# Reading the moving operand from the last column to the first in the three-product matmuls of a hybrid decoder layer

## What is computed

```python
h = rms_norm(x)                       # (512, 1024)
z = h @ w_in                          # w_in: 1024 x 6696, columns of all heads and of four gates
o_a, o_b, o_c, o_d = sparse attention, pooling, gated chunks, stick-breaking attention   # 256 wide each
proj = einsum('bsnw,nwd->bsnd', stack(o), w_branch)
x = x + sum_n(sigmoid(gate_n) * proj_n) @ w_out
h = rms_norm(x)
x = x + (silu(h @ w_ffn_gate) * (h @ w_ffn_up)) @ w_ffn_down      # 2816 hidden channels
```

## Time and profile before

| | us |
|---|---|
| median of 3 runs (773.85 to 774.11) | 774.07 |
| span of the profiled execution, first to last instruction | 772.3 |
| PE busy / PEld busy | 767.1 / 680.1 |
| DVE busy | 564.4 |
| ACT busy | 392.0 |
| POOL busy | 102.4 |
| chain that ended last: PE's share | 98% |

### The profile page before, as it was taken

How to read it: one execution, slowest core, us unless ns; L and a number is a source line. 1 busy time by engine, 2 the same in 40 slices (tenths; PEclk the granted TensorE clock), 3 DMA queues, 4 the chain that set the end, 5 groups by cost and what they waited for, 6 DMA issues and landing times.

```text
span 772.3 us, 11546 instructions
## 1 busy us (share of the span) xinstructions
PE 767.1 (99%) x4582; PEld 680.1 (88%) x4582; DVE 564.4 (73%) x796; ACT 392.0 (51%) x589; POOL 102.4 (13%) x126
## 2 busy tenths in 40 slices
PE   8999999999999999999999999999999999999998
PEld 8988888888888888888888899999889999999886
DVE  5536988878788965334435799889989888887991
ACT  6645545356573564443334465555544555555430
POOL 7100040457203211211310000000000000000000
PEclk9999999999999999999999999999999999999999
DMA  8362213221223221513234054335073333338202
GB/s 276 105 190 71 93 55 110 84 82 55 69 95 109 68 96 56 218 55 112 107 129 152 20 179 146 101 98 217 0 250 110 106 110 110 109 109 284 98 28 82
DMA packets 66629, 87.72 MB, mean 114 GB/s; under 512 B 1988, under 2 KB 52496, under 8 KB 66576
## 3 DMA queue, kind: packets, MB, share of 16 engines
q1 hardware_dynamic: 65680, 85.86, 34.0%
q0 software_dynamic: 752, 0.99, 0.5%
q10 hardware_dynamic: 144, 0.13, 0.0%
HBM read 81.21 MB, written 4.19 MB: 111 GB/s over the span
## 4 chain that ended last, share of the span: by engine, by line
PE 98%; issue 1%; POOL 1%; ACT 0%; DVE 0%; DVEq 0%; POOLq 0%
PE bank L2054 17%; PE bank L2056 17%; PE bank L2055 17%; PE bank L2499 9%; PE bank L2501 9%; PE bank L2500 9%; PE bank L2564 5%; PE bank L2560 5%; PE bank L2562 5%; PE bank L2327 1%; PE bank L2162 1%; PE bank L2297 1%; PE bank L2286 1%; PE bank L2318 1%; PE bank L2234 1%
## 5 line engine op out<-in xcount | busy, mean ns | idle before, releaser
L2054 PE MATMUL bank<-h_hi,w_hi 128*128 128x512 f32 (+1 forms) x368 | 139.9, 380 | 0.1
L2056 PE MATMUL bank<-h_hi,w_lo 128*128 128x512 f32 (+1 forms) x368 | 138.2, 376 | 0.0
L2055 PE MATMUL bank<-h_lo,w_hi 128*128 128x512 f32 (+1 forms) x368 | 138.1, 375 | 0.0
L1317 DVE TENSOR_TENSOR w_lo<-raw,w_hi 128x2048 fp32r<-128x2048 f32 x36 | 84.8, 2360 | 53.7 <-ACT w_hi L774 45.8
L2499 PE MATMUL bank<-t_hi,w_hi 128*128 128x256 f32 x320 | 89.6, 280 | 0.0
L2501 PE MATMUL bank<-t_hi,w_lo 128*128 128x256 f32 x320 | 89.4, 279 | 0.0
L2500 PE MATMUL bank<-t_lo,w_hi 128*128 128x256 f32 x320 | 89.4, 279 | 0.0
L2056 PEld LDWEIGHTS bank<-h_hi,w_lo 128*128 128x128 f32 x368 | 69.2, 188 | 12.8
L2054 PEld LDWEIGHTS bank<-h_hi,w_hi 128*128 128x128 f32 x368 | 69.2, 188 | 12.5 <-issue 0.4
L2055 PEld LDWEIGHTS bank<-h_lo,w_hi 128*128 128x128 f32 x368 | 69.3, 188 | 12.2
L774 ACT ACTIVATE w_hi<-raw 128x2048 fp32r<-128x2048 f32 x34 | 65.2, 1923 | 15.6 <-PE bank L2056 14.4
(11 more groups left out here) (305 smaller groups left out, 1804.5 us busy)
## 6 DMA issues: line engine op xcount, KB each, us to landing
raw<-in_w_in_dram SPq DMA_DIRECT2D x26, 1024.0 KB, 5.1
raw<-in_w_ffn_gate_dram SPq DMA_DIRECT2D x11, 1024.0 KB, 5.2
raw<-in_w_ffn_up_dram SPq DMA_DIRECT2D x11, 1024.0 KB, 5.2
raw<-in_w_ffn_down_dram SPq DMA_DIRECT2D x7, 1024.0 KB, 4.9
raw<-in_w_branch_dram SPq DMA_DIRECT2D x4, 1024.0 KB, 4.9
raw<-in_w_out_dram SPq DMA_DIRECT2D x4, 1024.0 KB, 4.8
b<-in_w_ffn_down_dram SPq DMA_DIRECT2D x4, 1024.0 KB, 6.7
x_sb<-in_x_dram SPq DMA_DIRECT2D x4, 512.0 KB, 6.2
```

The costliest lines, as they stand in the source:

```text
L1317: vec.tensor_tensor(w_lo[:, at], raw[:, c % 2, 0:n], w_hi[:, at].bitcast(F32), ALU.subtract)\
L2054: mm(dst, l_hi, r_hi, start=start, stop=False)
L2055: mm(dst, l_hi, r_lo, start=False, stop=False)
L2056: return mm(dst, l_lo, r_hi, start=False, stop=stop)
```

## The change

`three` turns the destination and the moving operand round, where the moving operand has two dimensions (so not in `pair_tile`), and `down_stage` does the same in its own three matmuls. Column 511 is read first and column 0 last, and column j of the product still lands in column j of PSUM. The stationary operand is as before, and so are all waits, counts, transfers and other engines' work. `wino_chunk` is not touched.

```diff
             def three(dst, l_hi, l_lo, r_hi, r_lo, start, stop):
 
+                if len(r_hi.shape) == 2:
+
+                    dst, r_hi, r_lo = dst[:, ::-1], r_hi[:, ::-1], r_lo[:, ::-1]
                 mm(dst, l_hi, r_hi, start=start, stop=False)
                 mm(dst, l_hi, r_lo, start=False, stop=False)
                 return mm(dst, l_lo, r_hi, start=False, stop=stop)
@@
                             w = slice(w_at(c) + k * HALF, w_at(c) + (k + 1) * HALF)
-                            mm(bank[banks[t]][:, :], l_hi[:, k, rows], w_hi[:, w], start=anew and k == 0, stop=False,
+                            mm(bank[banks[t]][:, ::-1], l_hi[:, k, rows], w_hi[:, w][:, ::-1], start=anew and k == 0,
+                               stop=False, skip_group_check=True)
+                            mm(bank[banks[t]][:, ::-1], l_hi[:, k, rows], w_lo[:, w][:, ::-1], start=False, stop=False,
                                skip_group_check=True)
-                            mm(bank[banks[t]][:, :], l_hi[:, k, rows], w_lo[:, w], start=False, stop=False,
-                               skip_group_check=True)
-                            ins = mm(bank[banks[t]][:, :], l_lo[:, k, rows], w_hi[:, w], start=False,
+                            ins = mm(bank[banks[t]][:, ::-1], l_lo[:, k, rows], w_hi[:, w][:, ::-1], start=False,
                                      stop=k == tiles - 1, skip_group_check=True)
                         ins.then_inc(S["down_tile"], 1)
```

## The result

| | before | after |
|---|---|---|
| median, us | 773.96 (4 runs) | 784.56 (4 runs) |
| ratio, 95% interval | | 1.0136 (1.0122 to 1.0151) |
| span of the profiled execution, us | 772.3 | 782.6 |

The change makes the kernel 10.6 us slower. The page of after, against the earlier trace rows: PE has 10.2 us more of busy time, the clock is as full as before and the chain lies on PE for 99% (98% before).

What follows compares the result with a forecast made beforehand. PE was taken as the bound, through distances between instruction starts. 1878 x 6 = 11.3 us plus 432 x 1.8 = 0.8 gave 12.1 off the 772.3 span; with 1.8 outside it, 762 us, range 749 to 797.

Steps and rivals of the forecast that it cites:

- the second rival: Turned matmuls: reads running the same way stay together longer; +8 ns on 2310, 18 us, 792; half, 783; chance 0.18.
- What bounds the kernel: Whole kernel: PE busy 767.1 of 772.3 us, so time is the sum of distances between its instruction starts.
- no other engine takes part: First down stage is tightest: 1.3 us saved there against DVE's 3.9 free, so the whole gain reaches the end.
- The count: Matmuls turned in `three` and the down stages: 1878 of 512 columns, 426 us, and 432 of 256, 52 us.
- the term for 512 columns: 1878 turned matmuls in `three` and the down stages: -6 ns each from 227, 11.3 us saved.
- The term for 256 columns: 432 turned matmuls by `three`: from 120 to the seven-product chunks' 118.2 ns, -1.8 each, 0.8 us saved.
- Nothing changes: Turned matmuls: the 32 cycles are a constant price of changing weights, or the order isn't carried out; 774; chance 0.27.
- Much slower: Turned matmuls: downward read or write falls to half pace, 427 ns for 512 columns; +446 us, 1220; chance 0.12.
- faster, by 2 to 25 us: Whole kernel: the likeliest case, time 762, own range given as 747 to 772, chance 0.43.
- the bound for 256 columns: Turned matmuls of 256 columns: distance no lower than the 107 ns of a weight load, at most -13 ns.

Runs made afterwards that it cites:

- e8: The kernel before, all reads upward, with `h` moved by 192 bytes against everything else; 778.65 us, ratio 1.0061.
- the rows: Separate kernels, layer not computed, running rows of equal matmuls in various lays and read directions; 512 columns upward at distance 0 took 226.6 ns, downward 233.4.
- second kernel of rows: Rows again, layer not computed, with lays in 16-byte steps and 512 columns read by blocks; blocks of 64 backwards, each upward: 226.6 ns.
- first kernel of rows: Rows of 32 equal matmuls, layer not computed, varying lay in 64-byte steps, direction, width and stationary columns; 512 columns: up 226.6 ns, down 233.4.
- third kernel of rows: Rows of 256 columns upward in the seven-product chunks' operand order, after short rows of another kind; the same row took 117.7, 113.3 and 117.9 ns.
- e3: The kernel before, all upward, with f and t laid so seven-product weights start 64 bytes after the moving operand; 772.87 us, ratio 0.9976.

## Why the prediction was wrong

The forecast was 762 us, faster; it came out 784.6, slower and inside the stated range. It is the second rival, a little slower.

*What bounds the kernel* was right: PE alone, 98% before and 99% after, and the time is the sum of the distances. So was the statement that no other engine takes part: PE's waits grew by 0.2 us.

*The count* was right: 1878 turned matmuls of 512 columns and 432 of 256; their sums moved by 11.0 and -0.2 us, and the seven products by less than 0.2.

*The step that failed* is the sign of the term for 512 columns: -6 ns each, 11.3 us saved, where +5.9 in the mean and +6.6 in the steady stretches was measured, 11.0 us lost. The prediction reasoned that a weight load read from the last column and a moving operand turned the same way have one pass over each other in place of three, and so fewer meetings. That the place of the weights matters to the moving read was right for the upward one, and e8 and the rows show it; that one can count passes was a picture with nothing behind it. No row of a trace shows the direction of a weight load either; the prediction has it from the compiled instruction list. The second kernel of rows contradicts it: the moving operand read by blocks of 64 columns from the end runs downward over the whole tile, with the pattern of every 256 bytes kept, and costs nothing. And the excess doesn't shrink when a weight load reads a quarter of the columns. The term for 256 columns, -1.8, came out at -1.6 in the first kernel of rows (120.0 and 118.4) and at -0.5 over the layer's 432, 0.2 us in place of 0.8. The right sign there is luck, since it came from the same reasoning.

What should have carried more weight stood in the front of this text: the tiles were laid so that weights and moving operand start alike, and the one pair of 512 columns with another lay had 235 ns. The rival took its +8 ns from there. The indexer's weights start 64 bytes after its moving operand, and upward rows at 64 have 233.1 ns with no semaphore between, so some 6.5 of the 8 were the lay's. The rows say that the upward lay at 0 is one of three good ones in sixteen, so a change of the order of the read, with no reason why it should be good at 0 too, should have been expected to lose. The rival's size was close for 512 columns, but it had a loss for 256 as well, and there the change gave a little back.

*Nothing changes* rested on 13.3 ns for both widths as a constant. Upward at a distance of 0 it is one, for a third width too (384 columns, L108: 5.55/32 = 173.4 ns, 13.4 above their 160.0), but it doesn't hold for another lay or order, as the rows from 226.6 to 240 ns show. *Much slower*, half pace for a downward read, is out: 233.4 ns. "PSUM — Partial Sum Buffer" (Specifications) of the Trainium skill was weighed there with its sentence on non-contiguous patterns; with the write alone downward the time is 773.93 us, so a step of minus one isn't such a case here. For the read that sentence says nothing.

Two bounds of the prediction don't follow from its own terms, though nothing hangs on them: "faster, by 2 to 25 us" from 774 is 749 to 772, not 747 to 772, and the lower end of the range, 749, leaves out the bound for 256 columns (432 x 13 = 5.6 us).

*What stays open*: why many rows settle on multiples of 16 cycles (544, 560 and 576 for 512 columns, 272 and 288 for 256) and others don't (117.8 and 236.7 ns), why the distances repeat every 256 bytes, why fewer stationary columns don't help, and whether the downward read loses by meeting the weight load or by itself. The runs show which order of which read costs, not what part of the chip takes it. The other order of the weight load wasn't tried.

## What to carry to other kernels

In a kernel that is PE from end to end, look at the distance between starts, and set it against the columns: here 13 ns of 227 were no columns. In the rows of 512 columns this part went from 13 to 27 ns, by where in 256 bytes the moving operand lies against the next weights and in which direction it is read. Before a change of address, order or placement, measure rows of equal matmuls with both lays: one kernel of 425 us gave what an argument got wrong. But take its small differences with care: the rows' 113.3 ns carried over to the layer only in part. And keep the 16-byte pieces within each 256 bytes in rising order; the 256-byte stretches themselves went from the last to the first for nothing.

## What the runs showed of the hardware

- The moving read of `float32r` may go downward at nearly full pace: 233.4 ns for 512 columns against 226.6, 118.4 for 256 against 120.0. The PSUM write may go downward for nothing (773.93 us against 773.86).
- The distance between matmuls of 512 columns depends on the place of the next weights against the moving operand: 226.6 ns upward at 0, 233.1 at 64; downward at 128 it is 240 in the second kernel of rows and 236.6 in the first. It repeats after 256 bytes: in the first kernel the upward rows at 256 and 320 have 227.5 and 233.4.
- Blocks of 16 columns read in order, each downward inside, cost 266.6 ns, the dearest order tried.
- At the same lay there can be two steady rhythms, 113.3 and 117.8 ns for 256 columns at 64 bytes, and in the third kernel of rows what ran just before decided which. So gains of two changes need not add: e3 saved 1.1 us, the same edit on after 3.9. Whether e3's two heaps of times are these rhythms isn't shown, since no execution of the lower heap was profiled.
